# The attention's steps of a head pair spread over nineteen overlapped beats, and the last tile's heads and output weights moved differently

## What is computed

```python
# differential attention, per head: two halves of 32, two softmaxes
prob = softmax(where(visible, s, -inf)); w = prob[0] - lam * prob[1]
# stick-breaking attention
log_keep = where(earlier, log_sigmoid(-z), 0)
wts = where(earlier, exp(log_sigmoid(z) + (reverse_cumsum(log_keep) - log_keep)), 0)
h += concat(rmsnorm(diff) * 0.8, stick) @ w_out
# experts: per token 8 heads x top 16 of 128 x 128 product keys
idx, g = top_k(...); act = gelu(c . expert_u[idx]); h += sum(g * act * expert_v[idx])
h += (p @ w_ple) * sigmoid(rmsnorm(h) @ w_pgate); y = rmsnorm(h)
```

## Time and profile before

| | |
|---|---|
| three runs | 4136.44, 4135.24, 4115.4 us (median 4135.24) |
| the profiled execution | 4120.1 us, of which 4118.3 us span from first to last instruction |
| busy share of the span | PE 80%, DVE 71%, POOL 67%, ACT 29% |
| bytes moved | 1369.16 MB, 332 GB/s over the span |

### The profile page before, as it was taken

One profiled execution on the slowest core, in us unless ns is written; L12 is line 12 of the kernel. 1 busy time (PEld: TensorE's weight loads), 2 busy tenths in 40 slices (PEclk: granted clock), 3 DMA queues, 4 the chain that ended last, 5 costly groups with the idle time before them and its releaser, 6 DMA issues.

```text
span 4118.3 us, 32609 instructions
## 1 busy us (share of the span) xinstructions
PE 3305.2 (80%) x9404; PEld 1584.9 (38%) x9404; DVE 2909.3 (71%) x5623; ACT 1179.8 (29%) x2269; POOL 2743.2 (67%) x2355
## 2 busy tenths in 40 slices
PE   7869996777978787888788778877888887868877
PEld 3434443333424333443344334433443342323333
DVE  2276764877687678768776877697768676687775
ACT  2312331143124213421353135213531342111121
POOL 0014544777777777777777777777777766567774
PEclk9989998988989999999999999999999998889999
DMA  5347779899999999999999999999999999899996
GB/s 199 103 138 268 264 266 368 312 384 383 340 362 377 354 347 362 364 345 366 355 371 338 360 361 354 335 357 364 353 357 358 357 376 386 315 331 379 380 373 235
DMA packets 452608, 1369.16 MB, mean 332 GB/s; under 512 B 47696, under 2 KB 118224, under 8 KB 451408
## 3 DMA queue, kind: packets, MB, share of 16 engines
q0 software_dynamic: 331776, 1208.11, 78.2%
q1 hardware_dynamic: 95312, 135.89, 9.3%
q10 hardware_dynamic: 25344, 23.07, 1.6%
HBM read 1338.57 MB, written 28.31 MB: 332 GB/s over the span
## 4 chain that ended last, share of the span: by engine, by line
PE 34%; POOL 28%; DMA 12%; DVE 11%; issue 11%; ACT 4%; ACTq 0%; SPq 0%; POOLq 0%; DVEq 0%
POOL u_ring L648 14%; POOL v_ring L665 14%; PE sum_ps L845 12%; PE z_ps L740 6%; PE z_ps L788 6%; DMA u_ring<-expert_u_in,idx_tile 6%; DMA v_ring<-expert_v_in,idx_tile 5%; DVE u_ring L1579 3%; PE sum_ps L740 2%; PE z_ps L878 2%; DVE neg_max L1775 1%; DVE arena L1673 1%; PE out_ps L905 1%; DMA arena<-g_ffn_in 1%; PE z_ps L1044 1%
## 5 line engine op out<-in xcount | busy, mean ns | idle before, releaser
L845 PE MATMUL sum_ps<-v_ring,diag 128*128 128x512 f32 x3196 | 1707.1, 670 | 569.6 <-DMA v_ring<-expert_v_in,idx_tile 422.1
L648 POOL DMA_INDIRECT u_ring<-expert_u_in,idx_tile x1152 | 1362.7, 1183 | 693.5 <-DVE dots L1579 338.5
L1579 DVE CUSTOM_DVE_ANT_0 u_ring<-u_ring,c_rows 128x1024 f32<-128x1024 f32 x1152 | 1406.1, 1226 | 589.8 <-DMA u_ring<-expert_u_in,idx_tile 577.6
L665 POOL DMA_INDIRECT v_ring<-expert_v_in,idx_tile x1152 | 1333.1, 1157 | 351.5 <-issue 324.5
L845 PEld LDWEIGHTS sum_ps<-v_ring,diag 128*128 128x128 f32 x3196 | 621.3, 210 | 1393.6 <-DMA v_ring<-expert_v_in,idx_tile 699.1
L1228 ACT ACTIVATE diag<-ident,coef 128x128 f32<-128x128 f32 x799 | 291.3, 396 | 648.6 <-PE sum_ps L845 578.8
L1593 DVE SCALAR_TENSOR_TENSOR acc<-v_ring,coef,acc 128x1024 f32<-128x1024 f32 x344 | 443.1, 1288 | 8.8 <-DMA v_ring<-expert_v_in,idx_tile 8.5
L788 PE MATMUL z_ps<-weights,arena 128*128 128x512 f32 x768 | 342.4, 599 | 3.3 <-ACT arena L1190 3.3
L740 PE MATMUL z_ps<-weights,arena 128*128 128x512 f32 x576 | 261.4, 605 | 7.3 <-DVE c_rows L1881 3.7
L788 PEld LDWEIGHTS z_ps<-weights,arena 128*128 128x128 f32 x768 | 146.5, 193 | 182.3 <-issue 175.7
L1319 ACT ACTIVATE arena<-z_ps,neg_max 128x128 f32<-128x128 f32 (+7 forms) x128 | 94.8, 741 | 373.0 <-DVE neg_max L1775 372.9
(11 more groups left out here) (192 smaller groups left out, 3024.2 us busy)
## 6 DMA issues: line engine op xcount, KB each, us to landing
u_ring<-expert_u_in,idx_tile POOLq DMA_INDIRECT x1152, 6.4
v_ring<-expert_v_in,idx_tile POOLq DMA_INDIRECT x1152, 6.4
weights<-w_in_in SPq DMA_DIRECT2D x6, 2048.0 KB, 16.7
u_ring<-w_query_in SPq DMA_DIRECT2D x16, 512.0 KB, 4.7
weights<-w_out_in SPq DMA_DIRECT2D x2, 4096.0 KB, 24.0
weights<-w_query_in SPq DMA_DIRECT2D x1, 8192.0 KB, 52.5
qk_turned<-arena ACTq DMA_DIRECT2D x24, 256.0 KB, 6.6
arena<-x_all_in SPq DMA_DIRECT2D x9, 512.0 KB, 6.9
```

Source lines behind the costliest of these rows:

```text
L648: pool.indirect_dma_start(u_rows[r % U_RING][:, :], None, ins["expert_u"], bass.IndirectOffsetOnAxis(ap=idx_tile[:, e % 2, at:at + 1], axis=0)
L665: pool.indirect_dma_start(v_rows[g % V_RING][:, :], None, ins["expert_v"], bass.IndirectOffsetOnAxis(ap=idx_tile[:, e % 2, at:at + 1], axis=0)
L845: mm = nc.tensor.matmul(sum_ps[:, half * W:(half + 1) * W], diag[:, by_tensor[g] % DIAGS, :], v_rows[g % V_RING][:, half * W:(half + 1) * ...
L1579: nc.vector.tensor_tensor_reduce(row, row, c_rows[e % 2][:, :], 1.0, 0.0, ALU.mult, ALU.add, dots[:, s % 2, r % TOP:r % TOP + 1]).then_inc ...
```

## The change

Nothing is computed otherwise. The attention becomes one function `attend(e)` with a loop over five m: the last steps of pair m - 1 (product of head 2, both turns and the product of head 3) lie in beats 0 to 2 of pair m, the result's copy in beat 3; for the last pair they lie in the first beats of the routing half. Each group's turn and copy has a beat of its own. The routing steps move back by three beats at first, by two at the end (`gates` from 59 to 61). The samples' heads go from `s_out` straight into `mix`, and `w_out` is reloaded in two halves, the first as soon as the last cached keys are turned.

```diff
-            def store_sample(b):
+            def place_sample(b):
                 sp.wait_ge(s_taken, 2 * b + 2)
-                sp.dma_start(heads[b * S:(b + 1) * S, :], s_out).then_inc(s_stored, 16)
+                if b == 0:
+                    sp.wait_ge(opened, TP)
+                sp.dma_start(mix[b * S:(b + 1) * S, :], s_out).then_inc(s_stored, 16)
+            def reload_w_out(half):
+                sp.dma_start(w_out[:, 4 * half:4 * half + 4, :], ...).then_inc(out_w_in, 16)
...
-                store_sample(b - 1)
-            load_w_out()
-            sp.wait_ge(s_stored, 16 * B)
-            sp.wait_ge(opened, TP)
-            sp.dma_start(mix[:, :], heads).then_inc(mix_in, 16)
+                if b == B:
+                    sp.wait_ge(s_k_turned, 4 * B)
+                    reload_w_out(0)
+                place_sample(b - 1)
+            sp.wait_ge(s_mixed, 2 * B)
+            reload_w_out(1)
             load_tokens(TP)
...
+            def attend(e):                       # PE; m - 1 only if m, scores only if m < 4
+                for m in range(5):
+                    go(attend_at(e, m, 0))
+                    weigh_values(i, m - 1, 2, n - 1)
+                    turn_weights(i, m - 1, 3, n - 1, 0)
+                    attention_scores(i, 0, n)
+                    go(attend_at(e, m, 1))
+                    turn_weights(i, m - 1, 3, n - 1, 1)
+                    attention_scores(i, 1, n)
+                    go(attend_at(e, m, 2))
+                    weigh_values(i, m - 1, 3, n - 1)
+                    go(attend_at(e, m, 4));  attention_scores(i, 2, n)
+                    go(attend_at(e, m, 5));  attention_scores(i, 3, n)
+                    go(attend_at(e, m, 7));  turn_weights(i, m, 0, n, 0)
+                    go(attend_at(e, m, 8));  turn_weights(i, m, 0, n, 1)
+                    attention_scores(i, 4, n)
+                    go(attend_at(e, m, 9));  attention_scores(i, 5, n)
+                    go(attend_at(e, m, 10)); weigh_values(i, m, 0, n)
+                    turn_weights(i, m, 1, n, 0)
+                    go(attend_at(e, m, 11)); turn_weights(i, m, 1, n, 1)
+                    go(attend_at(e, m, 12)); weigh_values(i, m, 1, n)
+                    go(attend_at(e, m, 13)); turn_weights(i, m, 2, n, 0)
+                    go(attend_at(e, m, 14)); turn_weights(i, m, 2, n, 1)
...
+            def attend(e):                       # ACT; m - 1 only if m, the rest only if m < 4
+                    go(attend_at(e, m, 0));  take_weights(i, m - 1, 2, n - 1, 1)
+                    go(attend_at(e, m, 1));  take_weights(i, m - 1, 3, n - 1, 0)
+                    go(attend_at(e, m, 2));  take_weights(i, m - 1, 3, n - 1, 1)
+                    go(attend_at(e, m, 3));  take_out(e, m - 1)
+                    softmax_top(i, 0, m, n)
+                    go(attend_at(e, m, 4));  softmax_top(i, 1, m, n)
+                    go(attend_at(e, m, 7));  softmax_top(i, 2, m, n)
+                    go(attend_at(e, m, 8));  take_weights(i, m, 0, n, 0)
+                    softmax_top(i, 3, m, n)
+                    go(attend_at(e, m, 9));  take_weights(i, m, 0, n, 1)
+                    go(attend_at(e, m, 10)); log_term(i, 0, n)
+                    go(attend_at(e, m, 11)); take_weights(i, m, 1, n, 0)
+                    go(attend_at(e, m, 12)); take_weights(i, m, 1, n, 1)
+                    raise_stick(i, 0, n)
+                    log_term(i, 1, n)
+                    go(attend_at(e, m, 14)); take_weights(i, m, 2, n, 0)
+                    raise_stick(i, 1, n)
...
+            def attend(e):                       # DVE
+                    # maximum 0, 1, 2, 3 at beats 2, 3, 6, 7; subtract_half at 5 and 9
+                    go(attend_at(e, m, 11)); break_stick(i, m, 0, n)
+                    go(attend_at(e, m, 13)); break_stick(i, m, 1, n)
...
-                go(route_at(e, 4))
+                go(route_at(e, 7))
                 turn_heads(t)
-                go(route_at(e, 5))
+                go(route_at(e, 8))
                 project_heads(t, 0)
-                go(route_at(e, 7))
+                go(route_at(e, 10))
                 project_heads(t, 1)
...
-                go(route_at(e, 10))
+                go(route_at(e, 13))
                 square_tokens(t)
```

More of the change, by code:

```diff
@@ L80, in vector_rows, with attend_and_sum_experts @@
     return ((2, 6, 10, 14), (2, 6, 10, 13), (6, 13), ())[s - 4]
-def attend_and_sum_experts(nc, const, ins, qk_turned, new_rows, heads, summed, y):
+def attend_and_sum_experts(nc, const, ins, qk_turned, new_rows, summed, y):
     with ExitStack() as ctx:
@@ L796, in project_heads @@
                 pe.wait_ge(inT_done, 2 * t + 1)
-                pe.wait_ge(out_w_in, 16 if t < TP else 32)
+                pe.wait_ge(out_w_in, 16 if t < TP else 48)
                 product(w_out, n, n)
@@ L1068, in route_first @@
                     match(0, g)
-            for m in range(4):
-                attending_step(-1, m)
+            attend(-1)
             route_first()
@@ L1075, in _ @@
                 if e < TP - 1:
-                    for m in range(4):
-                        attending_step(e, m)
+                    attend(e)
                 else:
@@ L1329, in log_term, with take_weights @@
                 nc.scalar.activation(u, u, ACT.Ln, bias=const.one).then_inc(log_done, 1)
-            def take_weights(i, m, h, n):
-                if 4 * n + h:
+            def take_weights(i, m, h, n, g):
+                if g >= len(groups(i)):
+                    return
+                if g == 0 and 4 * n + h:
                     act.wait_ge(out_done, 4 * n + h)
-                for g, (a, z) in enumerate(groups(i)):
-                    act.wait_ge(w_turned, groups_before(i, m, h) + (g + 1))
-                    nc.scalar.copy(weights_turned(i)[:, a * P:z * P], group_ps[:, 0:(z - a) * P]).then_inc(wT_done, 1)
+                a, z = groups(i)[g]
+                act.wait_ge(w_turned, groups_before(i, m, h) + (g + 1))
+                nc.scalar.copy(weights_turned(i)[:, a * P:z * P], group_ps[:, 0:(z - a) * P]).then_inc(wT_done, 1)
             def take_out(e, m):
@@ L1520, in _ @@
                 go(route_at(e, 48))
-                go(route_at(e, 53))
+                go(route_at(e, 55))
                 exponents(choices_made(t))
```

304 lines of the change are left out of this document (154 added, 150 removed).

## The result

| | median, us | runs | from | to |
|---|---|---|---|---|
| before | 4130.82 | 19 | 4115.28 | 4139.02 |
| after | 4149.30 | 19 | 4135.91 | 4165.24 |

The change makes the kernel slower: the ratio of the times is 1.0055, 95% interval 1.0043 to 1.0067, some 23 us (the two medians lie 18.5 apart). The forecast was 4092 us, from a sum of 33 us of gain. The profiled execution of the changed kernel has a span of 4145.2 us, 26.9 more than before.

A forecast was written before the change was run, and what follows sets the result against it. Gathers bound narrow tiles' attention and the order of steps tile 7's; terms of 20 + 3 + 4 + 0 + 6 = 33 us off 4120.1 gave 4087, or 4094 against the runs' mean; predicted 4092, range 4050 to 4150.

The forecast's parts named there:

- Attention, 20 us of gain: Attention of tiles 3 to 7: 1.5, 4, 5, 7 and 2.5 us gained, at most 54 in all.
- So four waits of 2 replace 34.1 / 4 = 8.5 us a pair: Tile 7's attention: shorter DVE waits for scores, softmax and second stick replace longer score waits, gaining about 0.6 a pair.
- Routing, 3 us of gain: Routing half: 3 us gained, between -6 and 6; the sum-of-squares wait moves without shrinking, one step gets a beat more.
- All steps move back by three beats together: Routing: the same six beats stay from turning the heads to the sum of squares, so that wait does not shrink.
- Before block 0, 4 us: Ahead of block 0: overlapping pairs wins 4 of PE's 27.5 us idle, between -8 and 15.
- Block 0, nothing: Block 0's first half, 88% PE: the order adds no work, so 0, from -5 to 8.
- Block 7, 6 us: Block 7: DVE's 3.04 us wait for heads goes, the product's wait shrinks by one 2.9 us row; between 0 and 12.
- B: Rival: the stick part binds, sticks 2 beats apart and the second waiting for ACT; 45 us slower, 4172; chance 0.12.
- A: Rival: bytes bind anyway, gathers end each stage; only 0 to 15 us gained, 4112 to 4127; chance 0.27.
- C: Rival: all room won, 54 in attention, 15 before block 0, 12 in block 7; 4046; chance 0.09.
- D: Rival: each ACT table switch adds a 1.38 us drain, 22 us in the four widest tiles; about 4116; chance 0.02.
- under 5: Sign at tile 7: PE's waits for ACT's copies fall from 22.9 us to under 5.

The follow-up runs named there:

- stick_early: Changed kernel with ACT's Abs, Exp and Ln for the second head's stick ahead of the first head's last Exp, as before: ratio 0.9994.
- stick_at_14: Changed kernel with only DVE's second stick a beat later, at beat 14 as before the change; ACT's order as changed: ratio 0.9983.
- stick_queries: Changed kernel with ACT's second-head stick work ahead of the first head's last Exp, and routing's copy and first query product ahead of the gelu: 0.9945.
- heads_in_sbuf: Kernel before, with only the samples' heads going straight into the mixing tile and the output weights reloaded in two halves: ratio 1.0009.
- copy_behind: Kernel before, with ACT's copy of the turned tokens' second half moved from beat 14 to 16, behind the gelu: ratio 1.0108.
- stick_late: Kernel before, with the change's stick part alone: ACT's second-head log term behind the first head's last Exp, DVE's second stick at beat 13: 1.0037.
- three repairs: Changed kernel with ACT's early stick order, query product and its copy ahead of the gelu, and result's copy behind the second softmax: ratio 0.9915.

## Why the prediction was wrong

- **Attention, 20 us of gain: the step that failed is "So four waits of 2 replace 34.1 / 4 = 8.5 us a pair".** The sizes at tile 7 held (8.5 less 8 is 0.5 a pair and not 0.6, which changes nothing): scores 13.1 us (16 by the walk), softmax 7.7 (8), second stick 8.1 (8). The rule for adding them did not. I exchanged DVE's waits one for one, and took a wait of 1 or 2 us as covered by the u ring, but what a wait costs is what POOL does four beats later. By DVE's waits for scores, softmax and stick tile 7 should have gained 5 us (28.9 for 34.1); it lost 3. Scores are late between single dots, which the ring covers in part; the stick's wait lies between two sticks of 4.7 us each, where two dots have to feed four slots: in tile 7 8.1 us of DVE's waits there went with 20.6 of POOL's, and without them (stick_early) 5.2 of POOL's were left. The changed attention took 1190 us in tiles 2 to 7 for 1194 before. With the stick repaired it takes 1172 to 1177, and with the other repairs 1163 to 1170: the gain of 20 (its bounds were 0 and 54) was there, 3 to 4 of it in tile 2, which I gave nothing, and the stick part ate it.
- **By tile the forecast missed too.** In the mean of three kernels with the stick repaired (stick_early, stick_at_14, stick_queries) against three of the old order (before, heads_in_sbuf, copy_behind), tiles 2 to 7 gain 4.2, 3.5, -0.1, 3.0, 2.2 and 9.8 us. I gave 0, 1.5, 4, 5, 7 and 2.5. Tile 7's 2.5 had the stick's 8 us of waits in it; without them the walk gives 10, so its other terms held. Half of the room at 380 GB/s was too much for tiles 4 to 6: 16 forecast, 5 measured.
- **Routing, 3 us of gain: the step that failed is "All steps move back by three beats together".** They moved together, but past a thing that stays: the gelu at the end of each sixteen beats. Copy and first query product went from beat 14 to 17 and so across it. For the attention I had seen such a copy behind the gelu; in the routing I did not ask. Undoing both gave 19 us; the routing halves cost 1217 us in the mean of three kernels with the fault (after, stick_early, stick_at_14) and 1199 in five without it, against 1200 in the old order. So the term was 17 to 19 us of loss, and without the crossing 0 to 1 of gain. My bound of -6 came from the packed end of the half, where POOL waits 8.1 us over six tiles for 5.1 before.
- **Before block 0, 4 us: right in number, by luck.** Nine executions of the new order reach block 0 at 242.9 us in the mean, four of the old at 247.4. But the attention of tile 0, from the first score to the copy of the last result, gains 7 to 10 us (94.7 to 97.3 for 103.6 to 105.3), and the routing behind it loses some 5 (82.7 to 84.5 for 78.7 to 81.1), a term that I did not have. There PE stands 3.49 us for the normed tokens in all nine, 1.35 in all four, and the changed kernel then takes 1.97 us for their turn and 17.33 for the first query product where the kernel before took 1.09 and 14.81: the granted clock of this stretch is 0.92 for 0.98, so part of it ran at the lower of the clock's two levels (1.2 for 2.4 GHz).
- **Block 0, nothing: inside its bounds.** 582.3 us in the mean of nine executions of the new order, 577.9 in four of the old, some 4 us of loss (the bounds were 5 of loss and 8 of gain). The term was for the first half, which lost 1 (319.6 for 318.4). The second half takes 266.8 to 269.0 us in the three kernels of the new order with the late stick, 257.8 to 262.9 in the six with it repaired and 258.1 to 261.0 in the old order: its loss goes with the stick, though stick_late does not show it in the old order.
- **Block 7, 6 us: wrong, in two ways.** The 3.04 us for the heads went, yet the next dots had been waiting for rows anyway (2.45 us there before, 1.21 and 1.20 with the heads in place), so heads_in_sbuf measured 1.0009: between 3 us of gain and 10 of loss. The row that the product's wait was to lose did come, with the new beats of the routing: in nine executions the wait is 8.0 to 12.1 us on DVE and 5.0 to 9.0 on POOL, in four of the old order 12.2 to 12.8 and 10.6 to 12.3. The second half is 1.6 us shorter in the mean (237.5 for 239.1), too little to tell from nothing between single executions. What I had no term for is the first half, 4.6 us longer (221.9 for 217.3). It is not the reload (heads_in_sbuf 217.1). It goes with TensorE's granted clock there: five kernels at 0.92 and 0.93 take 220.5 to 224.8 us, the eight at 0.94 to 0.98 215.8 to 221.4; why the clock differs is open.
- **The rivals.** B named the mechanism, the place (beats 11 to 15) and the sign, and had 0.12. Its price of 45 us was too high (25 to 30 by the two repairs, 15 alone; its first term, 16 pairs between 2.1 and about 1 us, is 25 and not 22), and its condition that the early beats bring nothing did not hold. A and C are out: with the faults repaired the kernel gains, but 35 of C's 81 us. D, a drain with each table switch, is not seen: the Ln starts 0.01 us after the load's end (2972.19 + 1.28, then 2973.48). The Trainium skill, ScalarE: Activation LUTs, section "What ACT_TABLE_LOAD costs", puts a switch at 2.66 us; the trace does not agree, with 1.28 in both kernels.
- **The signs.** PE's waits for copies ahead of the turns fell to 2.5 us, but 11.2 came back ahead of the products, so "under 5" was half right. The score waits came out lower and not more in number (13.1 us in 6, for 15 to 20). "Tile 6 under 203 us" (210.2), "tile 2 unchanged" (178.1) and "routing within 4 us of 200.7" (205.5) were wrong; the last heads do land within 6 us (5.4). "POOL waiting for dots right after beat 11" was the sign for B, and it is what the trace shows. "Tile 7 under 205 us" came with the repairs. The median of 4149.3 lies inside the range by 0.7 us only, which is luck: the direction was wrong.

In sum, and roughly, since the terms come from different executions: gains of some 22 us in the attention and 4 before block 0, a stick that takes 25 to 30 (block 0's second half with it), a crossing that takes 19, and 3 more lost in block 7 make a loss of about the 23 us measured. The forecast of 4092 us is nearly what the change gives with three repairs (4092.9 median), and that is chance: some 10 of it are from the result's copy, which was no part of the forecast, and the routing and block 7 gave none of their 9.

## What to carry to other kernels

Find the engine that feeds the bound resource (here POOL, four slots ahead of DVE) and price each moved wait by what that engine then waits, not by the wait's own length: 8 us of waits between two long instructions of DVE took 15 from POOL here. When a group of steps moves together, list what does not move (the gelu of each sixteen beats) and see on every engine which steps change sides. Space two long steps by the time that the other engine needs between them; a beat of distance was worth some 30 us here.

## What the runs showed of the hardware

The bytes of tile 2 were not at their limit before: the stage that moved 380 GB/s moved 395 in the changed kernel, at a DMA share of 1.01 for 1.00. The stage bound that I took from it, 380 for all tiles, was a measured pace and no ceiling.
